# One layer's routing to experts: the choice by pairwise comparisons, the last rows' norm weights on GpSimd, the first unit's turns ahead of the last list, the weights' logits behind the lists

## The reference

```python
grp_prob = softmax(t @ w_rg + b_rg)
grp_p, grp_idx = top_k(grp_prob, 1)                     # one group of four
exp_logits = (t @ w_re + b_re).reshape(-1, 4, 4)
in_group = einsum('tg,tge->te', grp_onehot, exp_logits)  # the four logits of that group
top_logits, top_local = top_k(in_group, 2)              # two experts of four
weights = grp_p * softmax(top_logits)
...
out = out + einsum('tef,efd->td', silu(t @ w_gate) * (t @ w_up) * weight, w_down)
```

## Time and profile before

| | |
|---|---|
| median of 3 runs | 653.88 us (653.12 to 654.07) |
| the profiled execution | 654.05 us |
| its span | 652.3 us |
| TensorE matmuls busy | 629.6 us, 97% of the span |
| TensorE weight loads busy | 511.8 us, 78% |
| VectorE busy | 481.5 us, 74% |
| ScalarE busy | 393.5 us, 60% |
| GpSimd busy | 172.6 us, 26% |

### The profile page before, as it was taken

How to read it: one execution, slowest core, us unless ns; L and a number is a source line. 1 busy time by engine, 2 the same in 40 slices (tenths; PEclk the granted TensorE clock), 3 DMA queues, 4 the chain that set the end, 5 groups by cost and what they waited for, 6 DMA issues and landing times.

```text
span 652.3 us, 9545 instructions
## 1 busy us (share of the span) xinstructions
PE 629.6 (97%) x3492; PEld 511.8 (78%) x3493; DVE 481.5 (74%) x816; ACT 393.5 (60%) x680; POOL 172.6 (26%) x216
## 2 busy tenths in 40 slices
PE   7999999899999999999999997999999999999984
PEld 6788878777778878888888875788888888888763
DVE  5878995698523443534764688899999999998877
ACT  7538585446625333234532562688988998898743
POOL 7000005998000000000000001154745645546200
PEclk9999999999999999999999998999999999999998
DMA  8656543122621222134136944367778787975573
GB/s 263 196 160 207 149 81 110 53 65 67 150 84 50 65 83 82 29 87 107 65 130 238 359 176 154 102 203 264 247 263 273 220 296 232 314 263 164 200 279 129
DMA packets 76961, 108.53 MB, mean 166 GB/s; under 512 B 31863, under 2 KB 54464, under 8 KB 76786
## 3 DMA queue, kind: packets, MB, share of 16 engines
q1 hardware_dynamic: 64320, 99.76, 47.5%
q0 software_dynamic: 12480, 8.11, 4.2%
q10 hardware_dynamic: 114, 0.04, 0.0%
HBM read 123.90 MB, written 20.98 MB: 222 GB/s over the span
## 4 chain that ended last, share of the span: by engine, by line
PE 86%; DVE 7%; POOL 2%; DMA 2%; issue 1%; ACT 1%; SPq 0%; POOLq 0%; DVEq 0%; ACTq 0%
PE bank L1799 23%; PE bank L1801 22%; PE bank L1800 22%; PE bank L2274 3%; PE bank L1865 1%; DMA expert_rows<-expert_rows_hbm 1%; DVE rank_onehot L1637 1%; PE bank L1987 1%; PE bank L2011 1%; PE bank L1997 1%; DVE w_lo L1176 1%; PE bank L2290 1%; PE bank L2050 1%; PE bank L2174 1%; PE bank L1853 1%
## 5 line engine op out<-in xcount | busy, mean ns | idle before, releaser
L1799 PE MATMUL bank<-h_hi,w_hi 128*128 128x512 f32 x288 | 118.3, 411 | 0.0
L1801 PE MATMUL bank<-h_hi,w_lo 128*128 128x512 f32 x288 | 112.6, 391 | 0.0
L1800 PE MATMUL bank<-h_lo,w_hi 128*128 128x512 f32 x288 | 112.3, 390 | 0.0
L1511 DVE TENSOR_TENSOR gate_up_lo<-ew_raw,gate_up_hi 128x1024 fp32r<-128x1024 f32 x92 | 108.4, 1219 | 3.4 <-PE bank L1801 2.0
L1176 DVE TENSOR_TENSOR w_lo<-w_raw,w_hi 128x2048 fp32r<-128x2048 f32 x26 | 59.9, 2305 | 46.6 <-ACT w_hi L838 46.5
L770 POOL DMA_INDIRECT unit_tokens<-ffn_rows,row_index x23 | 27.7, 1206 | 249.5 <-DVE row_index L1645 238.8
L1053 ACT ACTIVATE gate_up_hi<-ew_raw 128x1024 fp32r<-128x1024 f32 x92 | 92.0, 1053 | 0.0
L1799 PE MATMUL bank<-gate_up_hi,unit_in_hi 128*128 128x512 f32 x184 | 75.8, 412 | 0.6 <-DVE unit_in_lo L1671 0.6
L1801 PE MATMUL bank<-gate_up_hi,unit_in_lo 128*128 128x512 f32 x184 | 72.2, 392 | 0.0
L1800 PE MATMUL bank<-gate_up_lo,unit_in_hi 128*128 128x512 f32 x184 | 71.8, 390 | 0.0
L1799 PEld LDWEIGHTS bank<-h_hi,w_hi 128*128 128x128 f32 x288 | 54.1, 188 | 13.2 <-issue 2.2
(11 more groups left out here) (409 smaller groups left out, 1284.8 us busy)
## 6 DMA issues: line engine op xcount, KB each, us to landing
w_raw<-in_w_in SPq DMA_DIRECT2D x16, 1024.0 KB, 5.8
ew_raw<-in_w_gate SPq DMA_DIRECT2D x32, 512.0 KB
ew_raw<-in_w_up SPq DMA_DIRECT2D x32, 512.0 KB
ew_raw<-in_w_down SPq DMA_DIRECT2D x32, 512.0 KB
expert_rows_hbm<-sub_product SPq DMA_DIRECT2D x16, 256.0 KB
w_raw<-in_w_out SPq DMA_DIRECT2D x4, 1024.0 KB, 5.0
expert_rows<-expert_rows_hbm SPq DMA_DIRECT2D x8, 512.0 KB, 7.3
x_T<-in_x SPq DMA_DIRECT2D x4, 512.0 KB, 5.5
```

The lines of the kernel that those rows point to most:

```text
L1511: dve.tensor_tensor(dst, eraw[slot][:, :], hi.bitcast(F32), ALU.subtract).then_inc(elo_done, 1)
L1799: pe.matmul(out_ap, lhs_hi, rhs_hi, start=first, stop=False)
L1800: pe.matmul(out_ap, lhs_hi, rhs_lo, start=False, stop=False)
L1801: return pe.matmul(out_ap, lhs_lo, rhs_hi, start=False, stop=last)
```

## The change

The choice is made by comparing each of four logits with the three others, at once for the group logits and for all four groups (20 rows of four for each token): six comparisons, one sum that gives each logit's place among its four, and marks where a place is below 2 in a group whose place is 0. The logits of the choice, which only the weights need, are formed in `weight_logits` behind the one-hot of list 4, and the slot weights in `choice_weights` behind `extra_units`. Their exponentials move on ScalarE behind unit 1's high parts, their turn and copy to unit 6. The last tile's rows are multiplied by the norm's weights on GpSimd (and half of tile 2's) and scaled on ScalarE, in place of turned copies that TensorE turned back. Unit 0's gather gets an index of its own from one instruction. TensorE forms list 4's codes behind the turns of unit 0, turns unit 1 between the halves of unit 0's product, and has more filler matmuls between the lists.

```diff
-                else:
-                    sp.wait_ge(choice_exp, ROW_SCALED)
+                if t >= TT - 2:
+                    sp.wait_ge(choice_exp, ROW_SCALED if t == TT - 1 else HALF_SCALED)
                 sp.dma_start(h_rows[t * P:(t + 1) * P, :], tx[t][:, :]).then_inc(rows_out, 16)
...
-                pool.wait_ge(ids_done, 1 + batch_of(c))
+                pool.wait_ge(ids_done, 2 + batch_of(c) if u else 1)
...
+            pool.wait_ge(x2_in, 80)
+            pool.wait_ge(y_done, 2 * TT - 1)
+            nc.gpsimd.tensor_tensor(tx[TT - 2][:, S:], y[:, TT - 2, S:], nffn[:, S:], ALU.mult).then_inc(pool_set, 1)
+            nc.gpsimd.tensor_tensor(last_n[:, 0:S], y[:, TT - 1, 0:S], nffn[:, 0:S], ALU.mult)
+            pool.wait_ge(y_done, 2 * TT)
+            nc.gpsimd.tensor_tensor(last_n[:, S:], y[:, TT - 1, S:], nffn[:, S:], ALU.mult).then_inc(pool_set, 1)
             pool.wait_ge(rows_out, 16 * TT)
...
-            act.wait_ge(hf_dve, TT)
-            last_features(1).then_inc(hf_act, 1)
+            act.wait_ge(pool_set, HALF_BY_NORM)
+            act.wait_ge(ffn_rooted, TT - 1)
+            act.activation(tx[TT - 2][:, S:], tx[TT - 2][:, S:], ACT.Copy, scale=rst[:, TT - 2:TT - 1]).then_inc(choice_exp, 1)
+            act.wait_ge(pool_set, LAST_BY_NORM)
             act.wait_ge(ffn_rooted, TT)
-            act.wait_ge(tt_ps, 2 * TT + 1)
-            for h in range(2):
-                ins = act.activation(tx[TT - 1][:, S * h:S * (h + 1)], ps[2 + h][:, :], ACT.Copy, scale=rst[:, TT - 1:TT])
-            ins.then_inc(choice_exp, 1)
-            act.wait_ge(choice_step, GD_IN)
-            act.activation(gex[:, :, :], gex[:, :, :], ACT.Exp).then_inc(choice_exp, 1)
-            act.wait_ge(choice_step, ED_IN)
-            act.activation(dif[:, :], dif[:, :], ACT.Exp).then_inc(choice_exp, 1)
+            act.activation(tx[TT - 1][:, :], last_n[:, :], ACT.Copy, scale=rst[:, TT - 1:TT]).then_inc(choice_exp, 1)
...
                 if u == 0:
+                    act.wait_ge(choice_step, GD_IN)
+                    act.activation(gex[:, :, :], gex[:, :, :], ACT.Exp).then_inc(choice_exp, 1)
+                    act.wait_ge(choice_step, ED_IN)
+                    act.activation(dif[:, :], dif[:, :], ACT.Exp).then_inc(choice_exp, 1)
+                    act.activation(warm[:, :], epsb[:, :], ACT.Silu)
+                if u == 6:
                     act.wait_ge(tt_ps, WEIGHTS_TURNED)
-                    act.activation(w12_f[:, :], ps[1][0:2 * TT, 0:P], ACT.Copy).then_inc(choice_exp, 1)
+                    act.activation(w12_f[:, :], ps[7][0:2 * TT, 0:P], ACT.Copy).then_inc(choice_exp, 1)
                     act.wait_ge(choice_exp, WEIGHTS_COPIED)
                     act.dma_start(wt_rows[:, :].rearrange("(r p) o -> r (p o)", p=P), w12_f[:, :]).then_inc(slots_out, 16)
...
-            ffn_norm(TT - 2, (1,))
-
-            def one_hot(oh, v, vmax, key):
-
-                link(dve.tensor_tensor(key, v, bc_last(vmax, EG), ALU.is_equal))
-                link(dve.tensor_tensor(key, key, bc_mid(prio[:, :], TT), ALU.mult))
-                link(dve.tensor_reduce(kmx[:, :], key, AX.X, ALU.max))
-                link(dve.tensor_tensor(oh, key, bc_last(kmx[:, :], EG), ALU.is_equal))
...
-            gl = lg[:, :, 0:NG]
-            link(dve.tensor_reduce(gmx[:, :], gl, AX.X, ALU.max))
-            dve.tensor_tensor(gex[:, :, :], gl, bc_last(gmx[:, :], NG), ALU.subtract).then_inc(choice_step, 1)
-            one_hot(goh[:, :, :], gl, gmx[:, :], gkey[:, :, :])
-            link(dve.tensor_tensor(eprod[:, :, :, :], lg[:, :, NG:].rearrange("p t (g e) -> p t g e", g=NG),
-                                   over_experts(goh[:, :, :]), ALU.mult))
-            link(dve.tensor_reduce(ig[:, :, :], eprod[:, :, :, :].rearrange("p t g e -> p t e g"), AX.X, ALU.add))
-            link(dve.tensor_reduce(m1[:, :], ig[:, :, :], AX.X, ALU.max))
-            one_hot(e1[:, :, :], ig[:, :, :], m1[:, :], ekey[:, :, :])
...
+            fours = lg[:, :, :].rearrange("p t (r e) -> p (t r) e", e=EG)
+            beat_f = beat[:, :, :, :, :].rearrange("p t r e f -> p (t r) e f")
+            rows_ = TT * (1 + NG)
+            for e in range(EG):
+                mine = fours[:, :, e:e + 1]
+                if e:
+                    ins = dve.tensor_tensor(beat_f[:, :, e, 0:e], fours[:, :, 0:e], mine.broadcast_to([P, rows_, e]), ALU.is_ge)
+                if e < EG - 1:
+                    ins = dve.tensor_tensor(beat_f[:, :, e, e:], fours[:, :, e + 1:], mine.broadcast_to([P, rows_, EG - 1 - e]), ALU.is_gt)
+            link(ins)
+            link(dve.tensor_reduce(place4[:, :, :, :].rearrange("p t r e -> p (t r e)"),
+                                   beat[:, :, :, :, :].rearrange("p t r e f -> p (t r e) f"), AX.X, ALU.add))
+            link(dve.tensor_scalar(goh[:, :, :], place4[:, :, 0, :], 0.0, None, ALU.is_equal))
+            in_group = place4[:, :, 1:, :]
+            by_group = over_experts(goh[:, :, :])
+            dve.scalar_tensor_tensor(selb[:, :, :, :], in_group, 2.0, by_group, ALU.is_lt, ALU.mult).then_inc(choice_step, 1)
+            dve.scalar_tensor_tensor(sel[:, :, :, :], in_group, 2.0, by_group, ALU.is_lt, ALU.mult)
+            dve.scalar_tensor_tensor(sel12[:, 0, :, :, :], in_group, 0.0, by_group, ALU.is_equal, ALU.mult)
+            link(dve.scalar_tensor_tensor(sel12[:, 1, :, :, :], in_group, 1.0, by_group, ALU.is_equal, ALU.mult))
...
                 codes = code_bank(b)[:, 3 * u0:3 * (u0 + n_u)].rearrange("p (u c) -> p u c", c=3)
+                if not b:
+                    dve.tensor_scalar(gidx[:, :], code_bank(0)[:, 3:4], code_bank(0)[:, 2:3], None, ALU.add).then_inc(ids_done, 1)
                 link(dve.tensor_scalar(idf[:, 0:n_u, :], codes[:, :, 0:2], -float(P), EMPTY, ALU.mult, ALU.add))
                 dve.tensor_tensor(ridx[:, u0:u0 + n_u, :], idf[:, 0:n_u, :], codes[:, :, 2:3].broadcast_to([P, n_u, 2]),
...
+            def weight_logits():
+
+                gl = lg[:, :, 0:NG]
+                dve.tensor_tensor(chprod[:, 0, :, :], sel12[:, 0, :, :, :].rearrange("p t g e -> p t (g e)"), lg[:, :, NG:], ALU.mult)
+                dve.tensor_tensor(chprod[:, 1, :, :], sel12[:, 1, :, :, :].rearrange("p t g e -> p t (g e)"), lg[:, :, NG:], ALU.mult)
+                link(dve.tensor_reduce(gmx[:, :], gl, AX.X, ALU.max))
+                dve.tensor_tensor(gex[:, :, :], gl, bc_last(gmx[:, :], NG), ALU.subtract).then_inc(choice_step, 1)
+                link(dve.tensor_reduce(m12[:, :, :].rearrange("p k t -> p (k t)"),
+                                       chprod[:, :, :, :].rearrange("p k t e -> p (k t) e"), AX.X, ALU.add))
+                dve.tensor_tensor(dif[:, :], m12[:, 1, :], m12[:, 0, :], ALU.subtract).then_inc(choice_step, 1)
+
+            def choice_weights():
+
+                dve.wait_ge(choice_exp, GD_OUT)
+                link(dve.tensor_reduce(gsm[:, :], gex[:, :, :], AX.X, ALU.add))
+                link(dve.reciprocal(gp[:, :], gsm[:, :]))
+                dve.wait_ge(choice_exp, ED_OUT)
+                link(dve.tensor_scalar(w12[:, 0, :], dif[:, :], 1.0, None, ALU.add))
+                link(dve.reciprocal(w12[:, 0, :], w12[:, 0, :]))
+                link(dve.tensor_tensor(w12[:, 0, :], w12[:, 0, :], gp[:, :], ALU.mult))
+                dve.tensor_tensor(w12[:, 1, :], w12[:, 0, :], dif[:, :], ALU.mult).then_inc(choice_step, 1)
...
             one_hots(4)
+            weight_logits()
             row_ids(3)
-            dve.wait_ge(choice_exp, GD_OUT)
...
-            dve.tensor_tensor(w12[:, 1, :], w12[:, 0, :], dif[:, :], ALU.mult).then_inc(choice_step, 1)
-            row_ids(4)
...
             split_in_lo(0)
+            row_ids(4)
...
                 if u == 0:
                     extra_units()
+                    choice_weights()
...
-            keep_busy(12)
+            keep_busy(9)
             pe.wait_ge(choice_step, SEL_DONE)
...
+                        n_c = 3 if b else 4
                         for t in range(TT):
-                            ins = pe.matmul(code_bank(b)[:, 3 * u:3 * u + 3], hot[b % 2][:, :, c0 + t], idv[:, t, u, 0:3],
+                            ins = pe.matmul(code_bank(b)[:, 3 * u:3 * u + n_c], hot[b % 2][:, :, c0 + t], idv[:, t, u, 0:n_c],
...
             keep_busy(6)
-            for b in range(EARLY):
-                row_codes(b)
+            row_codes(0)
+            keep_busy(6)
+            row_codes(1)
+            keep_busy(2)
+            row_codes(2)
+            keep_busy(2)
+            row_codes(3)
...
             unit_in(0)
+            row_codes(EARLY - 1)
             for u in range(UNITS):
-                if u + 1 < UNITS:
+                if 0 < u < UNITS - 1:
                     unit_in(u + 1)
-                if u == 0:
+                if u == 6:
                     pe.wait_ge(choice_step, WEIGHTS_SET)
```

(6 more changed lines are left out.)

62 lines of the change are left out of this document (17 added, 45 removed).

## The result

The changed kernel took 658.09 us (median of 7 runs, 656.70 to 661.48), the kernel before 653.88 (653.12 to 655.66): ratio 1.0075, 95% interval 1.0056 to 1.0093, slower by 4.2 us. Forecast were 655.5 and a range up to 657.5: the side was right, the size 2.6 us too small. The profiled execution took 658.09 us, with a span of 656.4.

The account below looks back on a forecast made before the run. VectorE's list of instructions was taken to set TensorE's start of unit 1. A first down product 1.35 us later plus 0.1 for the moved weights' turn made 1.45 us on 654.05: 655.5, range 653.0 to 657.5.

Parts of the forecast that it names:

- Choice: VectorE behind the last logits: new instructions take 1.54 us, so chosen_b starts 2.7 us earlier, 2.5 with contention.
- Contention: GpSimd's products beside VectorE's last norm ahead of the choice: cost 0 to 0.45 us on the chain, taken as 0.2.
- Unit 0's turns: TensorE's turns of unit 0 follow list 3's codes at 402.6; the gather allows them at the latest at 403.8.
- Turns take 1.0 us at full clock: Unit 0's turns on TensorE ahead of the first product, put at 405.7, 4.9 us of lead.
- third rival: Low clock over the lists also covers product 0: turns 0.8 longer, 1.5 lost, total about +2.9, 657.0; chance 0.10.
- first case: Lead lost behind unit 1's split and clock drops in the gap: 655.5, or 657 if low twice as long; chance 0.45.
- The order: Unit 1's turns between product 0's halves: VectorE's extra-unit chain waits behind unit 1's split, TensorE waits 4 us for its one-hot.
- 0.35 us earlier, not 4.9: Start of VectorE's extra-unit chain behind unit 1's split; expected sign: within 0.5 us of where it starts now.
- The clock in the gap: TensorE without wide matmuls for 5 us from 413.0 drops to half clock; first down product 1.35 us later than now.
- second case: Lead lost but no clock drop: 654.6, or 654.4 without contention, 654.9 with all of it; chance 0.32.
- by 413.0: When TensorE has finished product 0 and unit 2's turns, ahead of its 4 us wait for the extra list's one-hot.
- Weights: Six slot-weight instructions on VectorE behind the extra-unit one-hot, 1.11 us no wait covers; TensorE waits at the first down product.

Follow-up runs that it names:

- e12: Kernel before with the new pairwise choice alone, the weights' logits behind the row ids of list 0: 654.72 us, ratio 1.0015.
- e13: e12 with 1 filler matmul in place of 12 ahead of TensorE's matmuls on the choice: 652.01 us, ratio 0.9967 to the kernel before.
- e7: e1 with GpSimd's part undone (old way for the last rows, norm half back on VectorE), 9 fillers kept: 653.20 us, ratio 0.9990 to the kernel before.
- e1: Changed kernel with unit 1's turns put back ahead of product 0: 651.44 us, ratio 0.9980 to the kernel before.
- e15: e10 without GpSimd's part and with 1 filler in place of 9 ahead of the choice: 654.02 us, ratio 1.0000 to the kernel before.
- e11: Changed kernel, order kept, with more fillers ahead of product 0 and 16 in the wait for the first extra list: 655.38 us, ratio 1.0025 to the kernel before.
- e2: Changed kernel with VectorE's extra-unit chain and its one-hot ahead of unit 1's low parts: 653.38 us, ratio 1.0006 to the kernel before.
- e3: Changed kernel with exponentials behind unit 0's high parts and the slot weights behind list 4's indices: 658.20 us, ratio 1.0080 to the kernel before.
- e4: Changed kernel with 16 filler matmuls in TensorE's wait for the first extra list: 657.22 us, ratio 1.0056 to the kernel before.
- e16: Kernel before with the pairwise choice, GpSimd's part for the last rows and 9 fillers, no moves of order: 651.01 us, ratio 0.9965.
- e17: e16 with 12 fillers between the codes of the five lists: ratio 0.9969 to the kernel before, median 651.10 us.
- e6: e1 with exponentials and slot weights moved into idle time and eight more fillers on TensorE: 654.04 us, ratio 0.9998 to the kernel before.
- e10: Changed kernel with unit 1's turns ahead of product 0, extra-unit chain ahead of unit 1's low parts, weights in idle time, more fillers: 652.48 us, ratio 0.9989 to before.

## Why the prediction was right in direction and wrong in size

Behind the residual row (389.25 before, 388.06 after):

| point | forecast | measured | off |
|---|---|---|---|
| chosen_b | 5.45 | 5.39 | -0.1 |
| gather issued | 9.15 | 8.99 | -0.2 |
| unit 0's turns start | 13.35 | 14.06 | +0.7 |
| first product | 16.45 | 18.21 | +1.8 |
| unit 1's low parts done | 22.25 | 26.27 | +4.0 |
| first down product | 36.41 | 40.25 | +3.8 |

**Choice: right.** Forecast 1.54 us for the new instructions, measured 1.46 (391.99 to 393.45); and e12 and e13, with the choice alone, have it at 5.17.

**Contention: right in size.** GpSimd's three products have the same shape and took 2.37, 1.28 and 1.73 us, and VectorE's norm half beside the second and third 1.03 in place of 0.75. e12 against after, and e7 against e1, put the price of GpSimd's whole part on the choice at 0.22 us; 0.2 was booked. GpSimd's timeline after, to set beside the earlier trace rows:

```profile
385.72 2.37 POOL L807 TENSOR_TENSOR ffn_in_T<-y_T,norm_ffn_b 128x512 f32<-128x512 f32 x1 [223.30 <-DVE y_T L1531]
388.05 1.28 POOL L808 TENSOR_TENSOR last_rows_by_norm<-y_T,norm_ffn_b 128x512 f32<-128x512 f32 x1
389.29 1.73 POOL L810 TENSOR_TENSOR last_rows_by_norm<-y_T,norm_ffn_b 128x512 f32<-128x512 f32 x1
```

What the forecast missed is that this part also moves the store that can hold the gather (e13 to e15).

**Unit 0's turns: off by 0.7.** I let the codes of list 3 release them; the gather's landing did, within the bound I had named (5.4). The chain of work that ended last, after, has its length, from GpSimd's instruction to the turns:

```profile
397.05 5.02 DMA unit_tokens<-ffn_rows,first_token_rows
```

The Trainium skill (DMA: Bandwidth & Descriptors, the section on the anatomy of one SWDGE DMA) gives about 2.0 us plus the bytes at 436 GB/s, which for 512 KB would be an estimate of 3.2 us. This gather of 128 rows took 5.0, and the measurement decides.

**The step that failed** is "Turns take 1.0 us at full clock", and with it the half of product 0 at 2.8 us. The forecast gave no reason for the full clock there, though in the kernel before the turns had run at half clock. Turns took 1.97 us, and unit 1's turns began 5.06 us behind the product's start (411.33 - 406.27), at half rate up to 411.1. That is 1.0 + 2.3 us, and with the 0.7 it makes the 4.0 in the table. e11 shows that the clock is the cause: with it held, the same turns take 1.13 us and the same half 2.81, and to down falls by 3.92. How long the stretch lasts is not settled by the order: in the changed kernel, e2, e3 and e4, alike on TensorE up to there, the half took 5.06, 5.26, 4.14 and 5.26 us.

This was the third rival, at 0.10 and +2.9. Three things were wrong in it. Its chance: I held 25 fillers against it, but none of them stands behind 400.3, and six us pass from there to the first wide matmul. Its place: I set it beside the first case, as if only one stretch could come, though nothing excluded both. And its size: 0.8 for the turns and 1.5 for the half product, measured 1.0 and 2.3.

**The order: the mechanism right, the point in time not.** VectorE's chain for the extra units does wait for unit 1's split and the lead is lost there; e1 and e2 show it. TensorE waits 3.87 us for the extra list (forecast 4), and from unit 1's split to the down product pass 14.0 us (forecast 14.2). But the chain does not start "0.35 us earlier, not 4.9": it starts 3.7 us later behind the residual row (26.18 against 22.52), outside the 0.5 us that the forecast set as its own sign. The wait has the forecast length only because both of its ends moved by about 4 us. The runs divide the loss. All that the changed kernel has beyond e16 (the moves of order, the index of unit 0's own, the fillers between the lists) comes to 40.25 - 33.25 = 7.0 us to down. With the clock held it is 36.33 - 33.25 = 3.1 (e11), so half clock is 3.9 of it. By medians: 1.0075 to 1.0025 for the clock, 1.0025 to 0.9965 for the rest. And nearly all of the 7.0 hangs on one move: e1 undoes that alone, half clock over the turns included, and comes to 33.58.

**The clock in the gap: right in kind, a little too dear.** It fell behind 416, as forecast, though not in the gap but at 421.3, when product 1 had begun. Its price was 0.7 us (e4), against the 1.0 that the forecast put between its first and second case; VectorE's lateness covers the rest. Two terms of that part of the sum are wrong on their own rows: the codes' "another 0.2" (16 codes took 1.15 us at half clock and 1.12 at full), and "by 413.0", which adds up to 413.3 (405.7 + 5.6 + 1.0 + 1.0).

**Weights: 1.11 us on VectorE, right in place** (419.74 to 420.85), but no wait shows them (e3), since TensorE is later still.

**What stays open.** The last residual row came 1.2 us earlier after than before, and 0.4 to 1.3 us in e1 to e17 (387.92 to 388.89), with nothing that was changed ahead of it but GpSimd's first product (385.72), also where the code ahead of it is the old one (e12, e13). I have no second profile of the kernel before to say whether its 389.25 is scatter. It is why 5.2 us in the stretch became 4.0 between the two profiled executions (4.2 between the medians), and it flatters the forecast by luck: the miss is 2.6 us in time, but 3.8 in the stretch that the forecast worked out. The 655.38 us of e11, so near the forecast 655.5, don't support it either, for e11's clock never falls there.

## What to carry to other kernels

Work that fills a wait is worth more than its length: unit 1's turns cost nothing in the wait for unit 0's split, and moved behind it they delayed everything that VectorE has in line behind them. When a chain gets shorter, look for what was hidden under it: here fillers (e12), a store (e13) and the clock (after, e6) each took the gain, or part of it, in one of the runs. Two rivals that don't exclude each other need a case in which both come true. And where a clock falls in some executions and not in others, one profile for each kernel is not enough: read the mean clock of every execution beside its time (e10).

## What the hardware showed that I had not expected

- After, codes and turns followed one another almost without a gap from 402.1 to 405, and the clock stayed at 0.50 until product 0 had run for 4.8 us (in e3 2.8, in e2 6.0); in e16 it was back at about 407.3, under turns alone (3.38 us for 16).
- Wide matmuls (512 columns) start 0.43 us apart at half clock (408.02 and 408.45 in e2) and 0.23 at full.
- Waits of like length ended differently: 1.63 us in e10 with the clock kept, 1.64 us in e15 with the clock at 0.50 from 416.1 to 422.9.
- A GpSimd multiplication of 128x512 took 2.37, 1.28 or 1.73 us, in this order and within 0.02 us in every kernel that has the three. VectorE's rows beside them differ, which is likely the reason; no run takes these rows away.
